# The first four projection items split by halves of the contraction, with their first halves between the second and fourth modulation piece

## What is computed

```python
mod = (jax.nn.silu(c) @ w_ada + b_ada)[:, None, :]
sh1, sc1, g1, sh2, sc2, g2 = jnp.split(mod, 6, axis=-1)
h = rms_norm(x, norm1_g) * (1 + sc1) + sh1
z = h @ w_in
a_val, a_gt, b_u, b_v, c_b, c_c, c_h, gates = jnp.split(z, [...], axis=-1)
a = a_val * jax.nn.sigmoid(a_gt)
```

## Time and profile before

| | |
|---|---|
| median of 3 runs | 1573.9 us (1573.7 to 1575.39) |
| the profiled execution | 1574.6 us |
| its span, first to last instruction | 1572.8 us |
| TensorE (PE) busy | 1532.8 us |
| VectorE (DVE) busy | 1235.4 us |
| ScalarE (ACT) busy | 795.1 us |

### The profile page before, as it was taken

How to read it: one execution, slowest core, us unless ns; L and a number is a source line. 1 busy time by engine, 2 the same in 40 slices (tenths; PEclk the granted TensorE clock), 3 DMA queues, 4 the chain that set the end, 5 groups by cost and what they waited for, 6 DMA issues and landing times.

```text
span 1572.8 us, 24371 instructions
## 1 busy us (share of the span) xinstructions
PE 1532.8 (97%) x9619; PEld 1330.4 (85%) x9619; DVE 1235.4 (79%) x1711; ACT 795.1 (51%) x878; POOL 385.7 (25%) x316
## 2 busy tenths in 40 slices
PE   6999999999999999999999999999999999999994
PEld 5788888878889999999999995888888888888882
DVE  4668887756747988895655558999999999999996
ACT  4222332335333213323233346787788877887775
POOL 0353000000000000001100202247655554444531
PEclk9999999999999999999999999999999999999997
DMA  9976322425334322232423487999999999999976
GB/s 333 323 214 210 89 80 87 148 75 158 121 94 148 121 81 84 72 96 84 126 76 88 124 284 282 401 406 403 397 396 402 401 392 382 380 389 390 385 277 242
DMA packets 220851, 363.35 MB, mean 231 GB/s; under 512 B 20358, under 2 KB 169934, under 8 KB 195640
## 3 DMA queue, kind: packets, MB, share of 16 engines
q1 hardware_dynamic: 196906, 323.19, 56.6%
q0 software_dynamic: 23184, 36.43, 7.9%
q10 hardware_dynamic: 646, 2.15, 0.4%
HBM read 363.01 MB, written 32.08 MB: 251 GB/s over the span
## 4 chain that ended last, share of the span: by engine, by line
PE 91%; DVE 3%; DMA 3%; SPq 1%; ACT 1%; issue 1%; DVEq 0%; POOL 0%; POOLq 0%; ACTq 0%
PE z L3142 17%; PE z L3144 17%; PE z L3143 17%; PE z L963 7%; PE z L965 7%; PE z L964 7%; PE z L980 3%; PE z L982 3%; PE z L981 3%; PE q L3030 2%; PE q L952 2%; DVE wl L1401 1%; DMA w_raw<-in_w_in_dram 1%; PE q L3056 1%; PE q L971 1%; DMA yt<-x_rows 1%
## 5 line engine op out<-in xcount | busy, mean ns | idle before, releaser
L1401 DVE TENSOR_TENSOR wl<-wr,whr 128x2048 fp32r<-128x2048 f32 x190 | 428.4, 2283 | 0.0
L3142 PE MATMUL z<-h_hi,w_hi 128*128 128x272 f32 (+1 forms) x1232 | 400.1, 325 | 0.0
L3144 PE MATMUL z<-h_hi,w_lo 128*128 128x272 f32 (+1 forms) x1232 | 396.2, 322 | 0.0
L3143 PE MATMUL z<-h_lo,w_hi 128*128 128x272 f32 (+1 forms) x1232 | 395.1, 321 | 0.0
L727 ACT ACTIVATE whr<-wr 128x2048 fp32r<-128x2048 f32 x190 | 359.9, 1911 | 52.9 <-PE z L965 51.6
L2319 DVE TENSOR_TENSOR w_lo<-w_raw,w_hi 128x1024 fp32r<-128x1024 f32 (+1 forms) x169 | 179.5, 1063 | 132.5 <-ACT w_hi L2014 132.3
L3142 PEld LDWEIGHTS z<-h_hi,w_hi 128*128 128x128 f32 x1232 | 231.7, 188 | 19.4 <-issue 3.8
L3144 PEld LDWEIGHTS z<-h_hi,w_lo 128*128 128x128 f32 x1232 | 231.4, 188 | 15.9
L3143 PEld LDWEIGHTS z<-h_lo,w_hi 128*128 128x128 f32 x1232 | 231.8, 188 | 15.1 <-issue 0.2
L2508 DVE SCALAR_TENSOR_TENSOR conv<-a_in,parT,conv 128x512 f32<-128x512 f32 x360 | 193.6, 581 | 13.6
L963 PE MATMUL z<-whr,xTh 128*128 128x512 f32 x512 | 202.5, 396 | 0.0
(11 more groups left out here) (533 smaller groups left out, 2339.6 us busy)
## 6 DMA issues: line engine op xcount, KB each, us to landing
wr<-in_w_dram SPq DMA_DIRECT2D x198, 1024.0 KB, 10.5
w_raw<-in_w_in_dram SPq DMA_DIRECT2D x104, 512.0 KB, 3.8
w_raw<-in_w_branch_dram SPq DMA_DIRECT2D x48, 256.0 KB, 2.7
ada<-in_w_ada_dram SPq DMA_DIRECT2D x5, 2048.0 KB, 12.7
w_raw<-in_w_out_dram SPq DMA_DIRECT2D x16, 512.0 KB, 4.3
ada_h<-in_w_ada_dram SPq DMA_DIRECT2D x2, 2048.0 KB, 15.2
ada_u<-in_w_ada_dram SPq DMA_DIRECT2D x2, 2048.0 KB, 10.8
ada_m<-in_w_ada_dram SPq DMA_DIRECT2D x2, 2048.0 KB, 11.6
```

The costliest lines, as they stand in the source:

```text
L1401: return dve.tensor_tensor(out, a, b, op)
L3142: pe.matmul(out, w_hi[w][:, k, :], hi[:, k, t0:t1], start=(k == 0), stop=False)
L3143: pe.matmul(out, w_hi[w][:, k, :], lo[:, k, t0:t1], start=False, stop=False)
L3144: last = pe.matmul(out, w_lo[w][:, k, :], hi[:, k, t0:t1], start=False, stop=(k == kn - 1))
```

## The change

Items 0 to 3 get four banks (z[0] and z[1], banks 0 and 1) and are computed in two halves of the contraction: `first_half(n)` over k = 0 to 3, `second_half(n)` over k = 4 to 7. Their weights are loaded, rounded and split in halves too: first halves ahead of pieces 2 and 3 on the load queue, second halves behind piece 3. The order of the modulation pieces becomes scale, shift of k = 0 to 3, then scale, shift of k = 4 to 7, so that first halves need pieces 0 and 1 alone. first_half(0) and (1) stand ahead of ada_mm(2), first_half(2) ahead of mod_columns(2), first_half(3) ahead of ada_mm(3). The later small steps move back: ada 4 to behind item 3, ada 5 behind item 5, ada 6 behind item 7, ada 7 behind item 8, spatial_weights behind item 9; row_read(6) and mod_read(5) go into c_chunk(0), ws_read behind the second ahead of it.

```diff
-X_DVE = (0, 1, 4, 2, 3, 5, 6, 7)
+X_DVE = (0, 1, 2, 3, 4, 5, 6, 7)
+W_EARLY = 4
-ORDER = (2, 3, 0, 1, 4, 5, 6, 7, 8, 9, 10, 11)
+ORDER = (2, 0, 3, 1, 4, 5, 6, 7, 8, 9, 10, 11)
...
-        def zparts(s, g):
-
+        def a_bank(g, i):
+            return i if g == 0 and i < W_EARLY // 2 else 0
+
+        def zparts(s, g, b=0):
+
+            return [(z[s][:, b, 0:HALF], 0, HALF)] if g == 0 else \
                 [(z[s][:, 0, 0:H2], 0, H2), (z[s][:, 1, 0:HALF - H2], H2, HALF)]
...
-            for i in range(4):
-                load_ada(i)
-            ada_after = {2: (4,), WS - 1: (5,), WS + 1: (6,), WS + 3: (7,), WS + 7: (8, 9), WS + 10: (10,), WS + 13: (11,)}
+            def load_half(n, h):
+                kk = slice(CG * h, CG * h + CG)
+                sp.dma_start(w_raw[n][:, kk, :], cols_of(("a_gt", "a_val")[n % 2], n // 2)[:, kk, :]
+                             ).then_inc((rows_in[PT + n], w_in_sem[n])[h], 16)
+
+            load_ada(0)
+            load_ada(1)
+            for n in range(W_EARLY):
+                load_half(n, 0)
+            load_ada(2)
+            load_ada(3)
+            for n in range(W_EARLY):
+                load_half(n, 1)
+            parameter_rows()
+            ada_after = {WS - 1: (4,), WS + 1: (5,), WS + 3: (6,), WS + 4: (7,), WS + 7: (8, 9), WS + 10: (10,), WS + 13: (11,)}
             for g in range(2):
-                for n in range(GC0):
+                for n in range(0 if g else W_EARLY, GC0):
                     if n < C0:
                         load(g, n, cols_of(("a_gt", "a_val")[n % 2], n // 2))
                     elif n < B0:
                         load(g, n, cols_of(("c_h", "c_c", "c_b")[(n - C0) % 3], (n - C0) // 3))
                     else:
                         load(g, n, cols_of(("b_v", "b_u")[n % 2], (n - B0) // 2))
-                    if g == 0 and n == 2:
-                        parameter_rows()
                     if g == 0:
                         for i in ada_after.get(n, ()):
                             load_ada(i)
-                    if g == 0 and n == WS - 1:
+                    if g == 0 and n == WS + 1:
...
+            def w_round_half(n, h):
+                kk = slice(CG * h, CG * h + CG)
+                act.wait_ge((rows_in[PT + n], w_in_sem[n])[h], 16)
+                act.activation(w_hi[n][:, kk, :], w_raw[n][:, kk, :], ACT.Copy).then_inc(whi_ok, 1)
+
             def ahead(g, i):
 
                 n = NI * g + i + AHEAD
-                if n < 2 * NI:
+                if W_EARLY <= n < 2 * NI:
                     w_round(n // NI, n % NI)
 
             for t in range(PT):
@@ -2031,17 +2050,23 @@
                 act.activation(h_his[0][:, k, 0:HALF], xTr[:, k, :], ACT.Identity, bias=modT[:, k, 0:1],
                                scale=modT[:, KD + k, 0:1]).then_inc(hhi_ok, 1)
 
-            q_wait_read(act, "modT", 2)
-            for k in X_ACT[0:2]:
-                h_high(k)
-            w_round(0, 0)
-            for k in X_ACT[2:4]:
-                h_high(k)
+            w_round_half(0, 0)
+            act.wait_ge(xt_free, PT)
+            q_wait_read(act, "modT", 1)
+            h_high(0)
+            h_high(1)
+            w_round_half(1, 0)
+            h_high(2)
+            h_high(3)
+            w_round_half(2, 0)
+            w_round_half(3, 0)
             q_wait_read(act, "modT", 3)
-            for k in X_ACT[4:]:
-                h_high(k)
-            for i in range(1, AHEAD):
-                w_round(0, i)
+            h_high(5)
+            w_round_half(0, 1)
+            h_high(6)
+            h_high(7)
+            for n in range(1, W_EARLY):
+                w_round_half(n, 1)
...
-                        if g == 0 and i == 0 and k == 0:
+                        if g == 0 and i == 0 and k == 1:
                             ws_read()
...
-            def first_low(h):
+            def w_low_half(n, h):
                 kk = slice(CG * h, CG * h + CG)
-                dve.wait_ge(whi_ok, 1)
-                tt(w_lo[0][:, kk, :], w_raw[0][:, kk, :], w_hi[0][:, kk, :].bitcast(F32), ALU.subtract).then_inc((w0_ok, wlo_ok)[h], 1)
+                dve.wait_ge(whi_ok, W_EARLY * h + n + 1)
+                tt(w_lo[n][:, kk, :], w_raw[n][:, kk, :], w_hi[n][:, kk, :].bitcast(F32), ALU.subtract).then_inc((w0_ok, wlo_ok)[h], 1)
 
             def scale_fix(c0):
                 dve.drain()
@@ -2465,30 +2490,36 @@
             x_scale(2)
             x_scale(3)
             mod_read(1)
-            scale_fix(4)
             dve.wait_ge(xt_free, PT)
             x_raw(0)
             x_raw(1)
-            ada_copy(2)
-            for k in (4, 5, 6, 7):
-                x_raw(k)
-            mod_read(2)
+            dve.drain()
+            w_low_half(0, 0)
+            x_split(0)
+            x_split(1)
             x_raw(2)
             x_raw(3)
             dve.drain()
-            x_split(0)
+            x_split(2)
+            x_split(3)
+            w_low_half(1, 0)
+            ada_copy(2)
+            w_low_half(2, 0)
+            mod_read(2)
+            scale_fix(4)
+            w_low_half(3, 0)
+            for k in range(CG, KD):
+                x_raw(k)
             ada_copy(3)
-            x_split(1)
-            first_low(0)
             mod_read(3)
             dve.drain()
-            for k in X_DVE[2:6]:
-                x_split(k)
-            first_low(1)
-            for k in X_DVE[6:]:
-                x_split(k)
-            for i in range(1, AHEAD):
-                w_low(0, i)
+            x_split(4)
+            x_split(5)
+            w_low_half(0, 1)
+            x_split(6)
+            x_split(7)
+            for n in range(1, W_EARLY):
+                w_low_half(n, 1)
...
-                    if g == 0 and i == 3:
-                        row_read(6)
-                    elif g == 0 and i:
-                        ada_copy(3 + i)
+                    if g == 0 and i >= 2:
+                        ada_copy(2 + i)
...
-                        if i >= 2:
-                            mod_read(2 + i)
+                        if i == 3:
+                            mod_read(4)
...
-                        row_read(7 + i)
+                        row_read(7 + i if i else 6)
+                    if g == 0 and i == 0:
+                        mod_read(5)
...
+                    if g == 0 and i == 0:
+                        row_read(7)
                     ahead(g, i0 + 1)
...
-                    transposed(z[1][:, 1, 384:512], ident[:])
+                    transposed(q[1][:, 1, 384:512], ident[:])
...
+            def early_out(n):
+                return z[n % 2][:, a_bank(0, n // 2), 0:HALF]
+
+            def high_high(n, k):
+                return pe.matmul(early_out(n), w_hi[n][:, k, :], h_his[0][:, k, 0:HALF], start=(k == 0), stop=False)
+
+            def high_low(n, k, stop=False):
+                return pe.matmul(early_out(n), w_hi[n][:, k, :], h_los[0][:, k, 0:HALF], start=False, stop=stop)
+
+            def low_high(n, k, stop=False):
+                return pe.matmul(early_out(n), w_lo[n][:, k, :], h_his[0][:, k, 0:HALF], start=False, stop=stop)
+
+            def first_half(n):
+                pe.wait_ge(whi_ok, n + 1)
+                for k in range(CG):
+                    pe.wait_ge(hhi_ok, k + 1)
+                    high_high(n, k)
+                if n == 0:
+                    pe.wait_ge(w0_ok, 1)
+                    for k in range(CG):
+                        low_high(n, k)
+                for k in range(CG):
+                    pe.wait_ge(hlo_ok, k + 1)
+                    high_low(n, k)
+                if n:
+                    pe.wait_ge(w0_ok, n + 1)
+                    for k in range(CG):
+                        low_high(n, k)
+
+            def second_half(n):
+                if n == 0:
+                    pe.wait_ge(whi_ok, W_EARLY + 1)
+                    for k in range(CG + 1, KD):
+                        pe.wait_ge(hhi_ok, X_ACT.index(k) + 1)
+                        high_high(n, k)
+                    pe.wait_ge(hlo_ok, CG + 1)
+                    high_high(n, CG)
+                    high_low(n, CG)
+                    pe.wait_ge(hlo_ok, CG + 2)
+                    high_low(n, CG + 1)
+                    pe.wait_ge(wlo_ok, 1)
+                    for k in range(CG, KD):
+                        low_high(n, k)
+                    for k in range(CG + 2, KD):
+                        pe.wait_ge(hlo_ok, k + 1)
+                        last = high_low(n, k, stop=(k == KD - 1))
+                else:
+                    pe.wait_ge(whi_ok, W_EARLY + n + 1)
+                    for k in range(CG, KD):
+                        high_high(n, k)
+                        high_low(n, k)
+                    pe.wait_ge(wlo_ok, n + 1)
+                    for k in range(CG, KD):
+                        last = low_high(n, k, stop=(k == KD - 1))
+                last.then_inc(item_mm, 1)
+
+            pe.wait_ge(xt_free, PT)
```

(79 more changed lines are left out.)

4 lines of the change are left out of this document (1 added, 3 removed).

## The result

The changed kernel takes 1591.86 us (median of 5 runs, 1588.05 to 1593.14) against 1573.9: a ratio of 1.0101, 95% interval 1.0086 to 1.0116. It is slower, as forecast, but by 18 us and not by 8.2, and it lies above the range of 1577.5 to 1585. The profiled execution took 1588.05 for a span of 1586.2.

The account below looks back on a forecast made before the run. TensorE, busy 97% of the span, was taken as the bound. Beginning +0.5, wait before ada_mm(7) +3.1 and before ada_mm(8) +4.6 made +8.2 on 1573.9: 1582.1 us, range 1577.5 to 1584.5, or 1585 with one clock fall.

Parts of the forecast that it names:

- What bounds: TensorE, busy 97% of the span; whatever the beginning gains or loses is handed through to the end.
- The beginning, +0.5: Start through item 8: idle is moved, not removed, costing +0.5 us, within 1.5 either way.
- The balance of idleness: Beginning: new idle of 6.9 us against 5.8 replaced, a loss of 1.1.
- the forward count: Beginning: adding times item by item puts item 8's end at 94.5, as before, a loss of 0.0.
- ada_mm(7), +3.1: After item 8: TensorE waits for row_read(6), now behind ahead(8) and its chain; +3.1 us, bounds 2.5 to 3.6.
- ada_mm(8), +4.6: After item 10: its load, issued later because wsT shares its memory, lands late; +4.6 us, bounds 1.0 to 8.6.
- the clock falls: Rival: after the sparse start or 4.6 gap, work runs at half pace; 1.7 each, 1583.8 or 1585.5; chance 0.2.
- the sign that the prediction had named for being wrong: Behind the gaps, matmuls of 512 columns come every 0.45 us rather than 0.23.
- The two arguments against the rival: Against falling clock: only the execution's whole start was slow; gaps up to 1.72 us had not brought slow pace back.
- the waits were not hidden: Rival: ada_mm(7) and ada_mm(8) find their data, only the start counts; 1573.9 to 1576 us; chance 0.08.
- the start did not win: Rival: first halves fill the 4.97 us of gaps between 26.2 and 36.7; 1569 us at best; chance 0.06.
- the weight halves were not late: Rival: weight halves land after 28 us, holding TensorE before ada 2 for 1 to 3 more; 1583 to 1585; chance 0.04.

Follow-up runs that it names:

- e9: Changed kernel with row_read(6), mod_read(5) ahead of ahead(8), spatial_weights, ws_read back behind item 8, and unused transposes in the beginning's gaps: 1578.39 us.
- e13: e9 measured again, unedited: 1578.72 us.
- e1: Kernel before the change with only the late moves (ada 4 to 7, spatial_weights and the small reads), old beginning kept: 1584.85 us, ratio 1.0069.
- e2: Changed kernel with row_read(6) moved ahead of ahead(8) in c_chunk(0): 1585.45 us.
- e12: Changed kernel measured and profiled again, unedited: 1589.85 us.
- e11: Changed kernel, both late waits mended, early rounding of second weight halves, ada_mm(3) ahead of first_half(3), ada 2 loaded and computed before first halves: 1571.24 us.
- e6: Changed kernel with unused matmuls filling the waits before ada_mm(7) and ada_mm(8), and unused transposes in the beginning's gaps: 1584.06 us.

## Why the prediction was right and wrong

**What bounds:** right. What was lost before 130 us (14.3) stands unchanged at the end of the dense part. The sum itself gave 8.2 where the trace has 8.8 (1.5, 3.1 and 4.2) before any fall of the clock.

**The beginning, +0.5:** the step was right in its mechanism and 1.0 too low. e9 and e13 give 1.5 and 1.6 without falls of the clock. The balance of idleness (1.1) was nearer than the forward count (0.0), and at item 8's end, 1.2 late in e9, it was nearly exact; I had taken the middle. With the falls item 8 ended at 98.18 and not near 94.5. Its single times hold: first matmul 28.54 for 28.5, gap of 1.65 for 1.6.

**ada_mm(7), +3.1:** right. 98.18 to 101.43 is 3.25, of which the product of 0.15 was counted elsewhere: 3.1. Reading the old chain behind item 8 gave it to the tenth.

**ada_mm(8), +4.6:** right, 4.23 to 4.44 over the profiles of e1, e2, e12 and the changed kernel. The load took 8.4 from its issue at 112.66, where 8.8 was assumed.

**The clock:** the step that failed. The sum put the falls of the clock at nothing; "the clock falls" was a rival at 0.2, priced at one or two falls. The changed kernel's first profile has four, its second four as well, three of them in the same places, and the sign that the prediction had named for being wrong is there: four matmuls of 512 columns start at 31.68, and the next group starts at 33.39, so they come every 0.43. The price of one fall, 1.7, was about right: 14.3 less 1.5, 3.1 and 4.2 leaves 5.5 for four, 1.4 each.

The two arguments against the rival were wrong. "No gap up to 1.72 brought the slow pace back" was true of the trace of before, but it says nothing of 2.4 with thin work around it, or of 3 to 4, and it does not even hold for all shorter gaps: 1.65 with thin work behind it was followed by 0.66 and 0.50 in the first profile after. "Only the whole start of the execution was slow" was a misreading: in the kernel before, TensorE's last matmul ends at 1553.15, and behind it the granted clock is down:

```profile
1555.00:1560.00 5.00, 0.00 (x0) 0.00 (x0) 4.32 (x9) 3.53 (x6) 0.00 (x0) 0.53 0.88 338
```

No work is left there to be slow, but the fall behind idleness was to be seen. The Trainium skill, "TensorE: Matmul & The Clock Gate", Part 1, has idleness return the clock to 1.2 GHz. The traces agree behind most of the new gaps (0.50 to 0.66); the fall in the router section, with no gap over 0.81 in front of it, is not of that kind. The column that I had called doubtful (1.00 at a slow start) showed each of these falls.

Had I charged 1.7 to each of the four sparse places that my own sum had named, the forecast would have been 1573.9 + 8.2 + 6.8 = 1588.9: inside the single runs, and 3.0 below their median. Where those 3.0 lie no trace shows; the lower mean clocks of the longer runs suggest longer or further falls.

**The range** went up only to one fall above the forecast; it had no room for several at once, though the four sparse places were all in the sum. (Its lower end is 0.8 below what its two named terms give: 1573.9 - 0.5 + 3.1 + 1.8 = 1578.3. That changes nothing here.)

**The other rivals:** the waits were not hidden; the start did not win, but e11 shows that it can, with the gap filled; the weight halves were not late (ScalarE rounded the first at 27.08 without waiting).

## What to carry to other kernels

A wait of the bounding engine is paid twice when it lets the matrix clock fall: charge the stretch behind each new gap, at least in the range, for here one and the same gap brought a fall in one profile and none in another. And ask first what could run in the gap. Moving small steps out of a crowded start is not free either: for each one, follow what it waits for at its new place, and what its own issue (a load, a buffer's release) unlocks; the chains that the old trace shows at that place price it well. And before work is pulled ahead, find the moment at which its inputs exist, and put there only work that needs none of them.

## What the runs showed of the hardware that was not expected

The same wait does not always bring the clock down. 2.95 before ada_mm(7) left it at 1.00 in e1 and took it to 0.50 in the changed kernel; the 1.65 before second_half(0) was followed by 0.50 in the changed kernel's first profile and by 1.00 in its second (e12). One fall, in the router section, came in five profiles with no gap over 0.81 in the 50 us in front of it. So place and length of the falls vary from run to run. The time varies too: nine runs of the changed kernel spread from 1588 to 1593, the longest ones at the lowest mean clocks, while the two profiled ones agree in both waits to 0.04, and the four runs of e6, without slow stretches up to 130 us in its profile, lie within 1.2. Unused transposes held the clock as well as unused matmuls did (e6, 25 to 60 us).
